# The order of a head's loads from DRAM in a hybrid attention and mLSTM layer: v goes first, then k and q, then the mLSTM's v

## The reference

```python
xn = rms_norm(h, norm_mix_w)
proj = einsum('bsd,de->bse', xn, w_in)      # q, k, v | ml_q, ml_k, ml_v, i, f, ml_o | gates
# mixer A, 8 heads: two softmaxes for each head, rotary on 16 of the 64 dims of q and k
a = p[:, :, 0] - lam * p[:, :, 1];  oa = rms_norm(a @ v) * 0.8
# mixer B, 8 heads: a causal convolution of width 4 on ml_q, ml_k, then a chunkwise mLSTM
ob = sigmoid(ml_o) * rms_norm(mlstm(qm, km, vm, i, f))
h = h + (g0 * (oa @ w_proj_a) + g1 * (ob @ w_proj_b)) @ w_out
h = h + relu(rms_norm(h) @ w_ff1) ** 2 @ w_ff2
out = rms_norm(h)
```

## Time and profile before

| | |
|---|---|
| median of 3 runs | 2116.82 us (2115.84 to 2119.14) |
| the profiled execution | 2115.07 us, of which span 2113.4 us |
| mean granted TensorE clock | 0.989 |
| TensorE busy | 2015.2 us (95% of the span) |
| VectorE, ScalarE, GpSimd busy | 813.1 (38%), 809.3 (38%), 509.9 us (24%) |
| DMA | 202.55 MB, mean 96 GB/s |
| loads of k, q, v and the mLSTM's v | 8 each, 512 KB each |

### The profile page before, as it was taken

One profiled execution on the slowest core, in us unless ns is written; L12 is line 12 of the kernel. 1 busy time (PEld: TensorE's weight loads), 2 busy tenths in 40 slices (PEclk: granted clock), 3 DMA queues, 4 the chain that ended last, 5 costly groups with the idle time before them and its releaser, 6 DMA issues.

```text
span 2113.4 us, 26680 instructions
## 1 busy us (share of the span) xinstructions
PE 2015.2 (95%) x9742; PEld 1678.2 (79%) x9742; DVE 813.1 (38%) x1345; ACT 809.3 (38%) x1544; POOL 509.9 (24%) x272
## 2 busy tenths in 40 slices
PE   5889998999999899989999999999999999999997
PEld 4778877787888787878877888888888888888876
DVE  5636655556575656543311122242112112211213
ACT  4435554546464555544333233333113112212321
POOL 1111111112121121211113444422222212222163
PEclk9999999999999999999999999999999999999999
DMA  6562534434343425252355444111111111111133
GB/s 181 143 193 65 155 60 123 92 113 110 104 120 107 107 77 146 71 162 71 60 146 173 149 135 121 49 50 50 50 41 50 50 50 50 50 47 43 50 100 120
DMA packets 236408, 202.55 MB, mean 96 GB/s; under 512 B 34136, under 2 KB 198360, under 8 KB 236336
## 3 DMA queue, kind: packets, MB, share of 16 engines
q1 hardware_dynamic: 223840, 192.05, 33.0%
q10 hardware_dynamic: 12224, 8.72, 1.3%
q0 software_dynamic: 272, 0.79, 0.1%
HBM read 151.13 MB, written 50.40 MB: 95 GB/s over the span
## 4 chain that ended last, share of the span: by engine, by line
PE 74%; DMA 10%; ACT 6%; DVE 5%; issue 3%; SPq 1%; ACTq 1%; POOL 0%; DVEq 0%
PE gp L552 21%; PE gp L554 21%; PE gp L553 20%; DMA w_raw<-in_w_in 6%; DMA proj_d<-ev 3%; PE ob L702 2%; PE ob L703 1%; PE scores L653 1%; PE scores L655 1%; PE tr L716 1%; DVE mx L1319 1%; ACT pr L1017 1%; PE scores L735 1%; ACT ev L868 1%; DVE cst L1374 1%
## 5 line engine op out<-in xcount | busy, mean ns | idle before, releaser
L1546 POOL TENSOR_TENSOR w_lo<-w_raw,w_hi 128x1024 fp32r<-128x1024 f32 x160 | 387.1, 2420 | 1409.6 <-ACT w_hi L863 1409.5
L552 PE MATMUL gp<-r1h,w_hi 128*128 128x512 f32 x1664 | 661.7, 398 | 26.0 <-ACT ev L868 22.5
L554 PE MATMUL gp<-r1h,w_lo 128*128 128x512 f32 x1664 | 653.4, 393 | 0.0
L553 PE MATMUL gp<-r1l,w_hi 128*128 128x512 f32 x1664 | 653.2, 393 | 0.0
L552 PEld LDWEIGHTS gp<-r1h,w_hi 128*128 128x128 f32 x1664 | 316.1, 190 | 94.0 <-ACT ev L868 14.0
L554 PEld LDWEIGHTS gp<-r1h,w_lo 128*128 128x128 f32 x1664 | 315.3, 189 | 67.9
L553 PEld LDWEIGHTS gp<-r1l,w_hi 128*128 128x128 f32 x1664 | 316.4, 190 | 63.0 <-issue 0.2
L863 ACT ACTIVATE w_hi<-w_raw 128x1024 fp32r<-128x1024 f32 x160 | 168.6, 1054 | 376.0 <-PE gp L554 253.3
L552 PE MATMUL gp<-r2h,w_hi 128*128 128x512 f32 x768 | 303.3, 395 | 0.1
L554 PE MATMUL gp<-r2h,w_lo 128*128 128x512 f32 x768 | 301.1, 392 | 0.0
L553 PE MATMUL gp<-r2l,w_hi 128*128 128x512 f32 x768 | 298.4, 389 | 0.0
(11 more groups left out here) (253 smaller groups left out, 2109.5 us busy)
## 6 DMA issues: line engine op xcount, KB each, us to landing
w_raw<-in_w_ff SPq DMA_DIRECT2D x72, 512.0 KB, 4.0
proj_d<-ev SPq DMA_DIRECT2D x128, 256.0 KB, 2.6
w_raw<-in_w_in SPq DMA_DIRECT2D x56, 512.0 KB, 8.9
xtok<-in_x SPq DMA_DIRECT2D x16, 512.0 KB, 3.6
pr<-proj_d SPq DMA_DIRECT2D x16, 512.0 KB, 4.2
gt<-proj_d SPq DMA_DIRECT2D x32, 256.0 KB, 3.8
w_raw<-in_w_in SPq DMA_DIRECT2D x16, 256.0 KB, 8.9
xT_d<-xTs SPq DMA_DIRECT2D x8, 512.0 KB, 4.0
```

Source lines behind the costliest of these rows:

```text
L552: pe.matmul(gp[half][:], wh[slot][:, k, :], mh[:, k, t], start=(k == 0), stop=False)
L553: pe.matmul(gp[half][:], wh[slot][:, k, :], ml[:, k, t], start=False, stop=False)
L554: mm = pe.matmul(gp[half][:], wl[slot][:, k, :], mh[:, k, t], start=False, stop=(k == KT - 1))
L1546: pool.tensor_tensor(wl[slot][:], raw[slot][:], wh[slot][:].bitcast(F32), ALU.subtract).then_inc(w_split, 1)
```

## The change

v is issued first in `att_loads`; for it the wait on the head before's `nd_done` is put ahead of everything, and the wait for stored blocks there asks for three blocks (q, k, v) in place of two. Then follow k with its turned rows, q with its turned rows, and the mLSTM's v, as they were. No instruction is added or taken away but one wait.

```diff
                 for i in range(2):
-                    sp.wait_ge(st[i], 16 * (h * HB + 2))
-
+                    sp.wait_ge(st[i], 16 * (h * HB + 3))
+
+                wait(sp, nd_done, h)
+                sp.dma_start(pr[:, 0, :], head_src(h, 2)).then_inc(v_in, 16)
                 wait(sp, qi_ready, h)
                 sp.dma_start(kraw[:], head_src(h, 1)).then_inc(k_in, 16)
                 wait(sp, kt_done, h)
@@
                 for i in range(2):
                     sp.wait_ge(st[i], 16 * (h * HB + 5))
 
-                sp.dma_start(pr[:, 0, :], head_src(h, 2)).then_inc(v_in, 16)
                 sp.dma_start(pr[:, 1, :], head_src(h, 4)).then_inc(mv_in, 16)
```

## The result

The changed kernel takes 2123.02 us in the median of 7 runs (2117.5 to 2127.13); the kernel before, on the same chip, 2115.84 us in the median of 7 (2112.2 to 2121.07). The ratio is 1.0029, with a 95% interval of 1.0018 to 1.004: 6 us slower (4 to 8.5). The forecast was 2136, within 2119 to 2152. The sign is right and the time lies in the range, but of the 19.4 us that were summed only a third came.

The account below looks back on a forecast made before the run. It took the time from `nd_done` to the block-1 weights' landing as the bound at changes of head; 14.6 (six heads) + 1.8 (last head) + 3 (clock) = 19.4 us, giving 2136 us, range 2119 to 2152 (80%).

Parts of the forecast that it names:

- the smaller rival: At changes of head, block-1 weights land faster (8.4 us each) once ScalarE's writes are out of the way: 2120 us; chance 14%.
- the cover of two us: VectorE's turning of k: later rows still land two us before they are read, so cost 0.
- the first head: First head: no `nd_done` to wait for, the weights keep the same count of loads ahead, so cost 0.
- the issue (2.43 us): SyncE's time to issue k and its rows before the block-1 weights: 2.43 us a head, counted instead of the data.
- The step that failed: Changes of head: every SyncE issue between `nd_done` and the block-1 weights' landing is on the path; 14.6 us over six.
- The prediction's part on k: k and its rows move behind `nd_done`, 2.43 us a head; the last block's store waits for ScalarE either way.
- The clock, 3 us: TensorE's granted clock falls after longer waits at two more changes of head: 3 us, between 0 and 6.8.
- The last head, 1.8 us: Last head: issuing k and its rows delays the load of weights by 1.8 us, bounds 0 and 3.5.
- The place of v, 0 us: v moved to the front of SyncE's loads: one issue on either side, no change for the weights, counted 0.
- The slower rival: At changes of head, `oa_d` gets in ahead of the weights and the clock is lost each time: 2152 us; chance 12%.
- The faster rival: Weights land in under 8.2 us in the mean, backlog drained and clock kept: 2101 us, or 2109 at half; chance 7%.
- Nothing is moved: Chain misread: waits at the end of each change of head have other causes at the same instant: 2117 us; chance 5%.

Follow-up runs that it names:

- e11: Changed kernel with seven eighths of each load of k left out (all heads but the first): 2126.66 us, 1.0045 to the kernel before.
- e12: Changed kernel without k's four loads of turned rows (all heads but the first): 2113.24 us, 0.9994 to the kernel before.
- e6: Kernel before, with block-2 weights issued right behind the last block's stores instead of after their landing: 2101.37 us, 0.9937.
- e7: Changed kernel, with block-2 weights issued right behind the last block's stores: 2114.71 us, 0.9992 to the kernel before.
- e10: Changed kernel with the large loads (v, k, q, mLSTM's v) first and the eight small row loads last: 2124.42 us, 1.0039 to the kernel before.
- e2: Kernel before with only the wait on `nd_done` put ahead of all loads, so k is late and v keeps its place: 2139.95 us, 1.0111.
- e3: The changed kernel itself, run again beside others on one chip: 2122.16 us, 1.0042 to the kernel before.
- e13: e2 with ScalarE's store of `oa_d` issued 2.5 us later, beside that of `ob_d`: 2130.29 us, 1.0061 to the kernel before.
- e5: Changed kernel, with block-1 weights issued one block earlier, ahead of all of a head's loads: 2099.32 us, 0.993 to the kernel before.
- e1: Kernel before with v alone moved ahead of q behind `nd_done`, k and its rows left early: 2109.4 us, 0.9974.
- e4: Kernel before, with block-1 weights issued one block earlier, ahead of all of a head's loads: 2098.26 us, 0.9922.
- e8: e1 with block-1 weights ahead of all loads and block-2 weights right behind the stores: 2090.81 us, 0.9886 to the kernel before.

## Why the prediction was right in sign and wrong in size

**What held.** The weights are issued 5.88 us behind the first load (5.96 forecast). S1 moved by 2.6 us (2.43 forecast). Their landing stayed, 10.8 us in the mean, so the smaller rival, by which they would have passed faster, has no part in it, though its 2120 lies near the time. VectorE turns k 9.3 us behind `nd_done` in both kernels: the cover of two us was enough. The wait for v is gone. In the first head nothing moved: the block-1 weights landed at 141.3 us in both. The forecast took the issue (2.43 us) for the price and not the data (2.1); the times of e11 and e12 speak for that, though 1.1 us of S1 came back with the data in e11. The Trainium skill says that the sequencer's time is usually small beside the DMA (DMA: Bandwidth & Descriptors, section Issuing engines are not separate DMA queues). For these loads of 32 KB it is not: by an estimate from rows 3 and 8, 0.47 us of issue for each stand against 0.1 us of data at 307 GB/s.

**The step that failed** is the first one, before the sum: "What bounds the kernel at these places is thus the time from `nd_done` to the landing of the block-1 weights; every DMA that SyncE issues in between is on the path", and with it 6 x 2.43 = 14.6 us carried in full to the end. In the kernel before, the path of five of the six heads ends by the block-2 weights, whose split comes 4.29 us ahead of the first exponentials. These weights wait in SyncE's queue for the landing of the last block's store, which is issued at +8.2 us whatever stands before it. The prediction's part on k had this store, but only its issue, and not what its landing lets go. S1 moved by 2.6 us, S2 by 1.1, the first exponentials by 1.4. The chain of rows 4 didn't show it: it goes through a load, ScalarE and the store of the first emptied bank (10.39 us), and I took it as it stood. That store landed when ScalarE was already at the split of the block-2 weights, which the chain leaves out.

Rows 2 had the hint too: 18.4 us of waiting for the probabilities is a second wait behind the first, and I took its sum with the other (41 us, to grow to 57) where one grew and the other shrank (45). Six heads came to 8.5 us in one execution and 10.6 in the other, not 14.6, where S1 alone would have made 15.7. Run e6 shows the second chain by itself: 13 us are gained with S1 where it was. That the change costs more without it (e7, 11.6 us by the ratios) fits, but is not clear of noise.

**The clock, 3 us: of both signs, and not 3.** Counted as half the length of its stretches at 1.2 GHz, from the first `nd_done` to the seventh, the granted clock missed 15.4 us in place of 11.9, and it fell in five of the six heads in place of four. What came new are stretches of 3.4 us some 23 us behind `nd_done`, just after TensorE has stood still for the bank. One of them (after; the row's last columns are clock, DMA share, GB/s):

```profile
595.20:598.60 3.40, 3.40 (x9) 2.62 (x8) 3.31 (x4) 3.00 (x4) 0.00 (x0) 0.50 0.70 197
```

Where the second chain sets the end, such a stretch costs nothing. Where the first does, it goes with 0.8 us: over all traces here, the exponentials come 18.2 to 18.3 us behind S1 in the nine such heads with one stretch of 3.4 us, and 17.5 in nine of the ten without (the tenth, in e10, has 18.3). (The rule's 20.2, which is 18.4 for the exponentials, fits the heads with a stretch, and that is most of its error. In e2, which has up to 6.8 us of it in a head, it adds up to 5.8 us.) In the changed kernel that is 0.8 us in one head, and 0.2 in another. Against it, two stretches of 3.4 us that the kernel before had further back in the head (37 and 49 us behind `nd_done`) are gone in this execution, and just these two heads gave back 1.1 and 2.1 us of their delay. That is most of what was given back; in e3 only the first of the two is gone. The forecast had only the loss.

**The last head, 1.8 us: not in the end.** Its load of the weights landed 1.5 us later, counted from `nd_done` (42.5 and 41.0), as the forecast had it. But from the last `nd_done` to the end of the span it is 1219.1 us before, 1218.5 after and 1218.5 in e3. It was given back further on; the traces don't tell me where.

**The place of v, 0 us: two errors that cancelled.** I priced v's place at nothing for the weights and drew the low bound with 0.9 us. It is worth 2.4 us of S1 (19.8 in e2, 17.4 in e3). Against this, k behind `nd_done` costs 5.3 us of S1 and not 2.43 (14.5 to 19.8): 2.5 of issue and 2.7 of slower landing. The sum, 2.9 us, is close to the 2.43 for a reason that I didn't have.

**The slower rival.** Its price was `oa_d` getting in ahead of the weights. It is real in e2, as e13 shows, where it costs 1.7 us of landing by my estimate and 2.3 by the runs. In the change the store itself came later (landing 10.5 us in the mean, 9.2 before) and the weights didn't (10.8). The Trainium skill says that a DMA engine takes turns between its queues (DMA: Bandwidth & Descriptors, section Queues, rings and completion order); e2 against e13 agrees with it.

**The faster rival** had a store of ScalarE's drained out of the way of the weights, under 8.2 us of landing in the mean. No run here reached it (10.0 us at best behind `nd_done`, in e11, and 8.9 in e5, where the weights are issued ahead of all); what did make the kernel faster, v's place in e1 and the early weights in e4 to e8, it did not name.

**Nothing is moved.** The time is above the band of this rival, and the interval leaves 1 out. But its words, that the waits at the end have other causes which come to the same instant, were half of the truth: the block-2 weights are such a cause. It had 5%.

**Still open.** e1 gains 5.5 us, where S1 and S2 come only 0.4 us earlier in the mean, which makes 2 us over six heads. And the load of the block-1 weights at 344 us takes 13.1 to 18.4 us wherever it was read behind `nd_done`, where its five neighbours take 6.4 to 14.4 for the same bytes; no run here tells why.

## What to carry to other kernels

Before a delay is carried in full to the end, look for the wait that comes next behind it, and follow its own chain back: what it is gated by that the edit does not move is the part of the delay that is hidden. A shift of one wait into another (one row of the table of waits grows, the other shrinks) is the mark of it. The profile's chain gives one releaser for each piece; hold each against what the engine was busy with at that moment, and against the loads that landed just before. And a queue's issues of small DMAs are a cost like any other where an important load stands behind them: what can be issued while the queue waits anyway should stay there, and large loads should not stand together directly ahead of the one that matters.

## What the hardware showed that was not expected

- Four loads of 32 KB cost SyncE 1.9 us of issue time (and the load behind them 0.9 us of landing) and, by way of the weights behind them, six times over, 7 to 10 us of the kernel (ratio 0.9994 in e12 against 1.0029 and 1.0042); 448 KB of data in the same place cost no time that can be measured (e11), though the weights split 1.1 us later for them.
- A store of 512 KB on ScalarE's queue, issued 0.7 us behind a load on SyncE's, made that load land in 13.3 us (mean of six); issued 3.4 us behind, 11.0 (e2, e13). That holds with two loads of 512 KB directly ahead of it; with rows of q between them (the change) it landed in 10.8, with the store as close.
- A stretch of 3.4 us at the lower clock, 23 us behind `nd_done`, puts the first exponentials 0.8 us later where the first chain sets the end (17.5 to 18.3 us behind S1), and not at all where the second does.
